# The last two levels of a blocked triangular inverse as products of 32x32 blocks

## The reference

```
sa = einsum('bhvk,bhk->bhv', s, kk_t)
s  = s * w_t - sa[..., None] * b_t + v_t[..., None] * k_t
y  = einsum('bhvk,bhk->bhv', s, r_t)
```

```
gt = minimum(xe @ w_gate[e] + b_gate[e], LIMIT);  up = clip(xe @ w_up[e] + b_up[e], ...)
out = ((up + 1) * gt * sigmoid(ALPHA * gt)) @ w_down[e] + b_down[e]
```

## Time and profile before

| | us |
|---|---|
| median of 3 runs | 1164.1 (1163.79 to 1164.47) |
| the profiled execution, its own time | 1165.45 |
| its span in the trace | 1163.6 |
| lines 1271 and 1281, first start to the start of U(0) | 152.35 to 162.54 |
| scan's chunk loop and output projection, router | 162.54 to about 238 |
| experts | about 238 to the end |

### The profile page before, as it was taken

How to read it: one execution, slowest core, us unless ns; L and a number is a source line. 1 busy time by engine, 2 the same in 40 slices (tenths; PEclk the granted TensorE clock), 3 DMA queues, 4 the chain that set the end, 5 groups by cost and what they waited for, 6 DMA issues and landing times.

```text
span 1163.6 us, 16613 instructions
## 1 busy us (share of the span) xinstructions
PE 1122.2 (96%) x6608; PEld 480.4 (41%) x6608; DVE 529.1 (45%) x1123; ACT 212.3 (18%) x433; POOL 34.1 (3%) x47
## 2 busy tenths in 40 slices
PE   9999999999999999999999999999999999999997
PEld 7666786643333333333333333333333333333332
DVE  6999965337333333333333333333333333333333
ACT  3265642221111111111111111111111111110012
POOL 0002412000000000000000000000000000000000
PEclk9999999999999999999999999999999999999999
DMA  9724006999999999999999999999999999999995
GB/s 247 214 86 179 20 16 175 429 392 415 417 427 427 429 428 430 427 429 427 430 429 427 430 427 430 428 429 427 430 427 429 430 426 430 429 429 427 429 421 204
DMA packets 58587, 430.00 MB, mean 370 GB/s; under 512 B 16670, under 2 KB 29390, under 8 KB 34220
## 3 DMA queue, kind: packets, MB, share of 16 engines
q1 hardware_dynamic: 58288, 428.84, 89.7%
q10 hardware_dynamic: 260, 0.61, 0.2%
HBM read 424.92 MB, written 4.48 MB: 369 GB/s over the span
## 4 chain that ended last, share of the span: by engine, by line
PE 53%; DMA 29%; DVE 4%; issue 1%; ACT 1%; DVEq 0%; ACTq 0%
PE bank L2166 35%; DMA ring<-in_w_up_dram 26%; PE bank L2133 5%; DMA arena<-in_w_up_dram 3%; PE bank L2140 2%; PE bank L2086 2%; PE bank L1734 2%; DVE arena L2536 1%; DVE arena L2560 1%; PE bank L1312 1%; PE bank L1271 1%; PE bank L2174 1%; PE bank L2192 1%; PE bank L1320 0%; PE bank L278 0%
## 5 line engine op out<-in xcount | busy, mean ns | idle before, releaser
L2166 PE MATMUL bank<-arena 128*64 128x512 f32 x1540 | 344.2, 594 | 11.4 <-DMA arena<-in_w_up_dram 11.2
L2166 PE MATMUL bank<-ring,arena 128*64 128x512 f32 x1532 | 342.2, 594 | 11.8 <-DMA ring<-in_w_up_dram 11.0
L2166 PEld LDWEIGHTS bank<-arena 128*64 128x64 f32 x1540 | 108.0, 136 | 225.8 <-issue 197.9
L2166 PEld LDWEIGHTS bank<-ring,arena 128*64 128x64 f32 x1532 | 108.0, 137 | 225.2 <-issue 198.0
L2560 DVE TENSOR_TENSOR arena<-arena,bank 128x512 f32<-128x512 f32 x180 | 110.0, 680 | 0.0
L2549 DVE SCALAR_TENSOR_TENSOR arena<-bank,arena 128x512 f32<-128x512 f32 x31 | 23.3, 751 | 182.0 <-ACT arena L1928 182.0
L2536 DVE TENSOR_SCALAR arena<-bank 128x512 f32<-128x512 f32 x31 | 21.4, 692 | 179.9 <-PE bank L2174 179.9
L610 PE MATMUL bank<-arena,ring 128*128 128x336 f32 x352 | 102.5, 447 | 0.3 <-DVE arena L751 0.3
L2133 PE MATMUL bank<-arena 128*64 128x512 f32 x372 | 86.7, 599 | 4.3 <-DVE arena L2560 0.6
L1904 ACT COPY arena<-bank 128x512 f32<-128x512 f32 x31 | 18.2, 587 | 354.3 <-PE bank L2133 354.3
L610 PEld LDWEIGHTS bank<-arena,ring 128*128 128x128 f32 x352 | 65.8, 189 | 34.2 <-issue 2.9
(11 more groups left out here) (387 smaller groups left out, 785.5 us busy)
## 6 DMA issues: line engine op xcount, KB each, us to landing
ring<-in_w_gate_dram SPq DMA_DIRECT2D x32, 2048.0 KB, 29.8
arena<-in_w_up_dram SPq DMA_DIRECT2D x32, 2048.0 KB, 32.8
arena<-in_w_gate_dram SPq DMA_DIRECT2D x32, 2048.0 KB, 29.9
arena<-in_w_down_dram SPq DMA_DIRECT2D x31, 2048.0 KB, 35.4
ring<-in_w_down_dram SPq DMA_DIRECT2D x31, 2048.0 KB, 35.4
ring<-in_w_up_dram SPq DMA_DIRECT2D x29, 2048.0 KB, 32.9
ring<-in_w_in_dram SPq DMA_DIRECT2D x11, 1024.0 KB, 8.4
ring<-in_w_up_dram SPq DMA_DIRECT2D x11, 512.0 KB, 7.3
```

The lines of the kernel that those rows point to most:

```text
L2166: mm = M.matmul(bank[64 * hb:64 * hb + 64, b, :], tokens(cc), rows[:, 512 * hb:512 * hb + 512], start=(cc == 0), stop=(w3 == 2 and cc == K ...
```

## The change

- The operands of levels 4 and 5 are treated as 32x32 blocks, each product on 32 rows and 32 columns of the array (`rows32(i, b)`: block b of head side i). Blocks that are zero, or known to be unchanged, are no longer multiplied.
- Level 4: G4 is 32 products of 32x32 (the diagonal blocks alone), on four row groups; the new AT4 is 16 products, of block 0 alone; the new A is 32 products of a 32x32 block with 64 moving columns, written crossed to two banks (`A_BANK`). E4 is a mask over 256 columns (`clow32`), AT4 a copy of 256 columns.
- Level 5: X = 16 products (32x32, crossed, two banks), E5 = minus X as a plain VectorE operation over 256 columns without a mask, Y = 16 products of E5 with block 1 of A; Y is copied into the upper right block of `A` in two parts, partitions 0 to 31 by ScalarE and 64 to 95 by VectorE (`first_rows`, `second_rows`).
- ScalarE's first AT0 takes two activations for each p instead of four (`half2`).
- `level5_x(0)` waits for `wc_ready` and `wc5_ready`, since X now uses banks 0 and 1, where W lay. U of chunk 5 now goes to bank 5 and stands between X and Y in TensorE's order, with Y(0), Y(1) after it. U(0) waits for the row copies.
- Three small constants are built in the first stage (`clow32`, `half2`, and `same16` is now waited for).

```diff
-                V.tensor_scalar(same16, geq[:, 4, :], -1.0, 1.0, ALU.mult, ALU.add)
+                link(V.tensor_scalar(same16, geq[:, 4, :], -1.0, 1.0, ALU.mult, ALU.add))
+                V.tensor_tensor(clow32, clow[:, 0, 0:32], clow[:, 0, 32:64], ALU.add)
+                V.tensor_tensor(half2, same16[:, 0:32:16], same16[:, 32:64:16], ALU.add)
...
+        G_BANK, A_BANK, X_BANK, Y_BANK = (7, 6), (4, 2), (0, 6), (4, 6)
...
-                for b in range(4):
-                    last = nc.scalar.activation(ATall[:, 8 * p:8 * p + 8, b, :], ATcol[:, 8 * p:8 * p + 8, :], ACT.Identity,
+                for b in range(2):
+                    last = nc.scalar.activation(AT0[:, 8 * p:8 * p + 8, 16 * b:16 * b + 16], ATcol[:, 8 * p:8 * p + 8, :],
...
+            for p in range(2):
+                act.wait_ge(S["at_done"], p + 1)
+                nc.scalar.copy(AT4[p], tiles(G_BANK[p], 256)).then_inc(S["at_ready"], 1)
+                act.wait_ge(S["a_done"], p + 1)
+                nc.scalar.copy(tile_pairs(A[p].rearrange("p q j c -> p (q j) c")), tile_banks(A_BANK[p], C))\
+                    .then_inc(S["a_ready"], 1)
...
             act.wait_ge(S["u5_done"], 1)
-            negated(2, 1, 6).then_inc(S["un5_ready"], 1)
+            negated(2, 1, 5).then_inc(S["un5_ready"], 1)
+            for p in range(2):
+                act.wait_ge(S["a_done"], 3 + p)
+                nc.scalar.copy(A[p][0:32].rearrange("p q j c -> p (q j) c")[:, :, 32:64], tiles(Y_BANK[p])[0:32])\
+                    .then_inc(S["first_rows"], 1)
...
+            def level4_g(p):
+                pe.wait_ge(S["at0_ready"], p + 1)
+                pe.wait_ge(S["n_ready"], 4 * p + 4)
+                pe.wait_ge(S["kbtok_ready"], 6 - p)
+                for u in range(8):
+                    for i in range(2):
+                        for b in range(2):
+                            g = rows32(i, b)
+                            mm = M.matmul(tiles(G_BANK[p])[g, u, :], Nm[p][g, u // 4, u % 4, 32 * b:32 * b + 32],
+                                          AT0[g, 8 * p + u, :], start=True, stop=True)
+                mm.then_inc(S["g_done"], 1)
+
+            def level4_a(p):
...
+                for u in range(8):
+                    for i in range(2):
+                        g = rows32(i, 0)
+                        mm = M.matmul(tiles(G_BANK[p], 256)[g, u, :], A[p][g, u // 4, u % 4, 0:32], E4[p][g, u, :],
+                                      start=True, stop=True)
+                mm.then_inc(S["at_done"], 1)
+                pe.wait_ge(S["old_read"], 3 + p)
+                for u in range(8):
+                    for i in range(2):
+                        for b in range(2):
+                            g, at = rows32(i, b), C * (u // 2)
+                            mm = M.matmul(bank[rows32(i ^ (u % 2), b), A_BANK[p] + u % 2, at:at + C], E4[p][g, u, :],
+                                          A[p][g, u // 4, u % 4, :], start=True, stop=True)
+                mm.then_inc(S["a_done"], 1)
+
+            def level5_x(p):
+                pe.wait_ge(S["at_ready"], p + 1)
+                if p == 0:
+                    pe.wait_ge(S["wc_ready"], 1)
+                    pe.wait_ge(S["wc5_ready"], 1)
+                for u in range(8):
+                    for i in range(2):
+                        g, at = rows32(i, 0), 32 * (u // 2)
+                        mm = M.matmul(bank[rows32(i ^ (u % 2), 1), X_BANK[p] + u % 2, at:at + 32],
+                                      Nm[p][g, u // 4, u % 4, 32:64], AT4[p][g, u, :], start=True, stop=True)
+                mm.then_inc(S["g_done"], 1)
+
+            def level5_y(p):
+                pe.wait_ge(S["e_ready"], 3 + p)
+                pe.wait_ge(S["a_ready"], p + 1)
+                for u in range(8):
+                    for i in range(2):
+                        g = rows32(i, 1)
+                        mm = M.matmul(tiles(Y_BANK[p])[rows32(i, 0), u, :], E5[p][g, u, :],
+                                      A[p][g, u // 4, u % 4, 32:64], start=True, stop=True)
+                mm.then_inc(S["a_done"], 1)
...
-            level_g(5, 0)
-            level_g(5, 1)
-            level_a(5, 0)
-            level_a(5, 1)
-            pe.wait_ge(S["wc5_ready"], 1)
+            level5_x(0)
+            level5_x(1)
             pe.wait_ge(S["a0_ready"], 3)
-            pe.wait_ge(S["a_ready"], 2)
-            each(6, lambda i, j: A[2][side(i), 1, j, :], lambda i, j: Wc5[side(i), j, :],
+            pe.wait_ge(S["a_ready"], 1)
+            each(5, lambda i, j: A[2][side(i), 1, j, :], lambda i, j: Wc5[side(i), j, :],
                  64, C, True, True).then_inc(S["u5_done"], 1)
+            level5_y(0)
+            level5_y(1)
...
+            def first_level(p):
+                dve.wait_ge(S["g_done"], p + 1)
+                V.tensor_tensor(E4[p], tiles(G_BANK[p]), b2(clow32, 8), ALU.mult).then_inc(S["e_ready"], 1)
+
+            def second_level(p):
+                dve.wait_ge(S["g_done"], 3 + p)
+                V.tensor_scalar(tile_pairs(E5[p]), tile_banks(X_BANK[p], 32), -1.0, None, ALU.mult)\
+                    .then_inc(S["e_ready"], 1)
+
+            def second_rows(p):
+                dve.wait_ge(S["a_done"], 3 + p)
+                V.tensor_copy(A[p][64:96].rearrange("p q j c -> p (q j) c")[:, :, 32:64], tiles(Y_BANK[p])[64:96])\
+                    .then_inc(S["second_rows"], 1)
...
+            second_rows(0)
             dve.wait_ge(S["u5_done"], 1)
-            negated(2, 1, 6).then_inc(S["un5_ready"], 1)
+            negated(2, 1, 5).then_inc(S["un5_ready"], 1)
+            second_rows(1)
```

More of the change, by code:

```diff
@@ L153, in build @@
         sel2 = take(2, 32)
+        clow32, half2 = take(32), take(2)
+        assert cursor[0] <= mixer_start + 16832
         cursor[0] = mixer_start + 16832
@@ L970, in build @@
         Nm = [pair_tile(at_word(6720 + 512 * p, 512)) for p in range(2)]
-        E = [pair_tile(at_word(o, 512)) for o in (4736, 23424)]
+        E4 = [at_word(o, 8, 32) for o in (4736, 23424)]
+        E5 = [at_word(o, 8, 32) for o in (4992, 23680)]
         A = [pair_tile(at_word(20864 + 512 * p, 512)) for p in range(NP3)]
-        AT = [pair_tile(at_word(22400 + 512 * p, 512)) for p in range(2)]
+        AT4 = [at_word(22912 + 256 * p, 8, 32) for p in range(2)]
         B16 = 17 * 16
@@ L980, in build @@
         Aall = at_word(20864, 24, 4, 16)
-        ATall = at_word(22400, 16, 4, 16)
+        AT0 = at_word(22400, 16, 32)
         Wc, Wc5 = [at_word(30080 + 256 * n, NPAIR, C) for n in range(2)]
@@ L1027, in build, with tiles, tile_pairs, tile_banks @@
         OLD_BANK = (4, 5)
-        G_BANK, AT_BANK = (7, 6), (4, 5)
-        A_BANK = {4: (2, 3), 5: (4, 2)}
+        G_BANK, A_BANK, X_BANK, Y_BANK = (7, 6), (4, 2), (0, 6), (4, 6)
+        def tiles(b, o=0):
+            return bank[:, b, o:o + 256].rearrange("p (u c) -> p u c", c=32)
+        def tile_pairs(v):
+            return v.rearrange("p (x b) c -> p x b c", b=2)
+        def tile_banks(b, n):
+            return bank[:, b:b + 2, 0:4 * n].rearrange("p b (x c) -> p x b c", x=4)
         def scan_sp(sp):
@@ L1264, in scan_pe @@
             turn_kb(4)
[L1266 to L1304, removed]
-                    pe.wait_ge(S["a_ready"], 2)
-                    square_crossed(A_BANK[l][p], E[p], A[p]).then_inc(S["a_done"], 1)
+            def rows32(i, b):
+                return slice(64 * i + 32 * b, 64 * i + 32 * b + 32)
@@ new lines, in level4_a @@
+            def level4_a(p):
+                pe.wait_ge(S["e_ready"], p + 1)
+                pe.wait_ge(S["a0_ready"], p + 1)
+                for u in range(8):
[12 more added lines that the diff above has]
+                mm.then_inc(S["a_done"], 1)
@@ L1418, in scan_pe @@
                 if c < 4:
-                    pe.wait_ge(S["a_ready"], 3 + p)
+                    pe.wait_ge(S["first_rows"], p + 1)
+                    pe.wait_ge(S["second_rows"], p + 1)
                 if c == 0:
-                    pe.wait_ge(S["a_ready"], 4)
+                    pe.wait_ge(S["a_ready"], 2)
                 if c < 4:
@@ L1561, in scan_dve @@
             spread_a(0)
-            level(4, 0)
+            first_level(0)
             spread_a(1)
-            level(4, 1)
+            first_level(1)
             spread_a(2)
@@ L1570, in scan_dve @@
             z_affine(0)
-            level(5, 0)
-            level(5, 1)
+            second_level(0)
+            second_level(1)
             def negated(p, q, b):
```

20 lines of the change are left out of this document (8 added, 12 removed).

## The result

| | before | changed |
|---|---|---|
| median of 8 runs, us | 1163.9 (1163.3 to 1164.7) | 1167.6 (1167.0 to 1170.0) |
| profiled execution, us | 1165.45 | 1167.92 |
| its span, mean granted clock | 1163.6, 0.999 | 1166.1, 0.995 |

The ratio is 1.0033, with a 95% interval from 1.0024 to 1.0042: the changed kernel is 3.7 us slower by the medians. It was forecast to be 4.2 faster.

What follows compares the result with a forecast made beforehand. TensorE was taken to bound the inverse; its issue falling from 8.5 to 4.5 us, with hand-overs, shortened 10.19 to about 6.0, a gain of 4.2, taking the median from 1164.1 to 1159.9 us; range 1159.2 to 1162.6.

Steps and rivals of the forecast that it cites:

- Rival 4: At the experts' start: a slot or transfer, not TensorE, sets it, so the gain doesn't reach the end; 1163 us, 5%.
- PE is the bound: In the inverse: TensorE (PE) is busy 9.63 of 10.19 us and sets the time; other engines' work lies inside.
- PE's issue falls from 8.5 to 4.5: In levels 4 and 5: TensorE's issue time in us, summed over the product groups, before and after the change.
- Rival 2: In the inverse: TensorE is fed no faster than one record and its load per 14.7 ns; gain 2.6, 1161.5 us, 15%.
- rival 5: In both levels: records of different rows writing one bank take turns; 1172.4 us, slower from about 21 ns each, 4%.
- The prices of the groups: In both levels: issue per group, G4 0.51, AT4 0.51, A4 0.47, X 0.26, Y 0.51 us, each twice.
- rival 1: A4 gets only four parts at once, or small terms run long; gain 3.5, 1160.6 us, within the forecast's 62%.
- The hand-overs: Between TensorE, VectorE and ScalarE in the inverse: some 1.5 of the 6.0 us left after the change.
- the 11.2 us of the estimate: Issue of 448 records at a 25 ns floor between matmul starts; some 1.8 us slower than before.
- The new path leaves it idle for no more than 0.3 us at a time, so I count no change: TensorE's granted clock in the inverse: stays at 1.00 (2.4 GHz), no cost counted.
- GpSimd's first cast: Behind the inverse: starts near 157.2 us, 3.9 earlier, with first expert weights near 193.0 instead of 196.94.
- The first stage: At about 19 us: two added VectorE operations and a wait cost at most 0.5 us, taken in by a later wait.

Runs made afterwards that it cites:

- e3: Changed kernel with half of the products of all five groups left out (224 records, not the whole inverse); 1159.8 us, single run.
- e5: Kernel before with 32 extra unused 32x32 products (64 records) between the two first groups of level 4; ratio 1.0008 to the kernel before.
- e11: Changed kernel with unused filler products, two in level4_a(0) and four in level4_a(1); ratio 1.0037 to the kernel before.
- e4: Changed kernel with G4 and A4 back to 64x64 products, AT4, X and Y still 32x32, 320 records; ratio 1.0009 to the kernel before.
- e12: e4 with one unused product on 256 columns between the two groups of level5_y; ratio 0.9991 to the kernel before.
- e7: e4 with one unused product on 512 columns between the two groups of level5_y; ratio 0.9991 to the kernel before.
- e2: Changed kernel with A4 and X written straight instead of crossed, part of the computation altered; 1168.4 us, single run.
- e10: Changed kernel with half of both levels' products left out and one TensorE pause ahead of level5_x(0); 1164.0 us.
- e1: Changed kernel with 24 more 32x32 products (48 records) at the scan's start, 21 us before the inverse; 1168.6 us, single run.
- e8: Changed kernel with unused filler products, two ahead of level4_a's first block group and four ahead of level5_x; ratio 1.0023 to the kernel before.
- e9: Kernel before, 64x64 products, with two TensorE pauses, ahead of level_a(4, 0) and level_g(5, 0); ratio 1.0054 to the kernel before.
- e6: Kernel before, 64x64 products, with one TensorE pause ahead of level_g(5, 0); ratio 1.0011 to the kernel before.

## Why the prediction was wrong

**What bounds the inverse.** That TensorE sets it, and that what changes there reaches the end, was right: +1.6 at U(0) and +1.7 by the clock became +3.7 at the end, and in e3 -4.6 became -4.7. Rival 4 falls. "PE is the bound" left out its supply. The kernel before used 256 instructions in 3.7 us, the rate at which they come to the changed one, and its own trace shows the fetches (155.02, 158.83). I never looked at that queue.

**The step that failed** is "PE's issue falls from 8.5 to 4.5". It counts the array's time and not the number of instructions, which the change raises from 640 to 896: the supply of instructions stands in the sum at nothing. From G4(0) to U(0) the runs show:

| kernel | records | us | ns each |
|---|---|---|---|
| before | 336 | 10.19 | 30.3 |
| e5 | 400 | 10.80 | 27.0 |
| changed | 464 | 11.82 | 25.5 |
| e11 | 476 | 11.91 | 25.0 |
| e4 | 336 | 9.00 | 26.8 |
| e12 | 338 | 9.19 | 27.2 |
| e7 | 338 | 9.70 | 28.7 |
| e3 | 240 | 5.56 | 23.2, hand-overs among them |

(U of chunk 5 and the filling are counted.) Whatever the shapes, no kernel with more than 300 records got below 25 ns. The forecast had 6.0 us for these 464 records, 13 ns each. Rival 2 had the form, "PE is not fed faster", but took its size, 14.7 ns, from a group of 32 records, which are 64 instructions and come out of the stock; over the whole stretch a record takes nearly twice that. My own break-even for rival 5 was 21 ns per record: by that, 25 is slower.

**The prices of the groups** were near, where the instructions were at hand: both G4 1.28 (forecast 1.02), AT4 0.47 (0.51; 0.63 in e12), A4 about 0.7, from 58 records in 0.63 (0.47, so rival 1 in part), X 0.35 in e11 (0.26), Y 0.63 in e12 (0.51). Twice their sum is 5.6 in place of 4.5 (5.9 with e12's AT4), so with instructions for all the gain would have been about 2.8 to 3.1, an estimate from these rows. The hand-overs, 1.5, were right (e3).

**Rival 5** falls, though its sign was right: four row groups write one bank in G4 at 10.0 ns per record. Here the rule of the Trainium skill, TensorEngine Tiling (Array Packing), Restrictions and Gotchas, isn't borne out by this case. Nor is the floor of 25 ns in the Trainium skill, TensorE: Matmul & The Clock Gate, Part 1, as one for the whole engine; one for each of the four parts is not spoken against, since there 10.0 ns are 40. That the 11.2 us of the estimate stand close to the measured 11.8 is chance: the records come 10.0 ns apart, and then not at all.

**The clock.** "The new path leaves it idle for no more than 0.3 us at a time, so I count no change" rested on the failed step. With stops of 1.59 and 2.25 us it fell, and that was 1.7 of the 3.7 us.

**Behind and ahead.** GpSimd's first cast came at 161.92 (forecast 157.2), the first weights at 198.42 (193.0), since the first cast waits for E5(1), and that for X, behind the second stop. The first stage cost nothing: G4 starts at 152.34, before at 152.35.

The Trainium skill, Runtime: NRT & Kernel Launch, Instruction fetch mechanics, says that an engine's instructions are refilled in blocks of 16 KiB, 256 instructions, and that crossing into a new block is mostly hidden. The fetches here have that size, and the stops that distance. That the crossing is hidden, the trace bears out for the kernel before and not for the changed one, which stood 1.59 and 2.25 us.

## What to carry to other kernels

A product costs its time on the array and its instructions, here four for one in 32 bits (two records and two loads), and the second price appears only when there are many small ones in a row: count the instructions of a dense stretch, hold them against the fetches in the instruction queue (here 256 in about 3.7 us), and if the two are already near each other, make products wider, not smaller. A short row of records in a trace shows what the array can do, not what the stream can keep up. And where TensorE would stand as long as in the stops that brought the half clock here (1.30 us in e4, 1.59 and more elsewhere), price the clock behind the stop as well (1.7 us here); a product for nobody in that place can be cheaper than the stop, as in e12.

## What the hardware showed that I had not expected

- 32x32 products on four parts of the array start 10.0 ns apart over 128 records, into one bank.
- TensorE's instructions: 16 KB at a time, 0.9 to 1.4 us per fetch, TensorE going on 1.2 to 1.6 us after it landed, the next fetch 1.0 to 1.2 us after that (1.6 in e2). The three make the 3.7 us.
- The half clock outlasts its stop by several us: to 168 us in the changed kernel, to 167 in e4, to 164 in e10. It can also set in late: TensorE was at work again for 1.4 us (after), 1.3 (e1), 1.2 (e2), 0.6 (e8) and 1.4 and 0.3 (e9) when it fell.
- Stops of 1.29 (e6) and 1.30 us (e4) went differently, 1.00 and 0.50. e6 had 64x64 products around it and e4 small ones (e11's 1.16 at the full clock among small ones too), one profiled execution each; whether that made the difference wasn't settled.
- Some executions have a mean clock of 0.66 from 145 to 150 us, ahead of these levels (the profiled ones of e1, e7 and e8, where G4 starts at about 154.3 in place of 152.2 to 152.9). That may be a part of the scatter between runs of one kernel, and it is the reason why e7's and e8's levels are compared from G4(0) and not from the span's start.
